# Latent attention: who copies the rotated queries, casts the keys and splits the sparse outputs, and where the first half projection stands

## The chip, the core and the metric

The kernel runs on one core of a Trainium2 chip. The metric is the device time of one execution in microseconds; below it is the median of several runs. The engines named are TensorE (PE; PEld is its weight load), VectorE (DVE), ScalarE (ACT), GpSimd (POOL) and SyncE (SP), which issues most DMAs. TensorE's clock has two levels, 1.2 and 2.4 GHz; the profile shows the granted one as a share of the higher.

## The reference, cut to what matters

The kernel computes two transformer blocks. The first has two layers of feed-forward, token mixer, feed-forward on 512 tokens of 1024 channels; the second is a mixer of another kind with routed experts, and is not touched. The change lies in the token mixer of the first block, in the latent attention (MLA) and in what follows it:

```python
def mla_attention(q_nope, q_pe, k_nope, k_pe, v):
    scale = (MLA_NOPE + MLA_ROPE) ** -0.5
        ...
        s = (jnp.einsum('bqhd,bkhd->bhqk', qn, k_nope, ...)
             + jnp.einsum('bqhd,bkd->bhqk', qp, k_pe, ...)) * scale
        s = jnp.where(kpos[None, :] <= qpos[:, None], s, NEG)
        p = jax.nn.softmax(s, axis=-1).astype(v.dtype)
        return jnp.einsum('bhqk,bkhd->bqhd', p, v)
```

There are 8 heads. A query or key of a head has 64 plain columns and 32 rotated ones; the rotated key columns are the same for all heads. The sparse attention (NSA) of the same mixer is done before. The outputs of both are then projected, multiplied by gates, added and projected once more.

## The kernel before

**Precision.** Products in 32 bits are made of three products of rounded parts. A tensor x is split into a high part, which is x rounded (whi, othi, mla_...), and a low part, which is x minus its high part (wlo, otlo). The product is lo·hi + hi·lo + hi·hi, so each product half of four column blocks is twelve matmuls (`products`, L424).

**Weights.** They come as blocks of 128x1024. SyncE loads a block into one of two `raw` buffers once GpSimd has split the one before the last. ScalarE casts it to `whi` (`hi`, L619, recorded at L624). GpSimd subtracts for `wlo` (`splitter`, L2967) and counts w_ready. TensorE waits for that count. GpSimd runs through its blocks in a fixed order, so whatever stands ahead of a split on its queue delays it.

**The hand-over.** The end of the mixer's first part makes the queries and keys of all heads from 14 tiles (`MLA_TILES`). VectorE takes those with even number, ScalarE those with odd number. Tiles 4 and 6 are the rotated parts of all queries; VectorE rotates them into q_rot (L1435 to L1438, L1618). After tile 10, VectorE subtracts for the low parts of head 0 (L1631 to L1633), copies tile 12 (L1622), and then lets TensorE and ScalarE pass a meeting point (`sync_point`, L412). Before TensorE reaches that point it does the first 12 matmuls of a gate block.

**The units.** Head and query tile make 32 units: 8 heads, and in each head four query tiles (qt 0 to 3) whose scores reach over 128, 256, 384 and 512 keys. Four functions walk through them, one for each engine, by the same counter u. TensorE (`pe_units_whole`) at step u first does three matmuls of a gate block (`feed`, L469), then the scores of unit u (L882 to L884), the transposes of the probabilities of unit u-2 (L892), and the product with the values of unit u-3 (L903). The gate matmuls end with u = 27. VectorE (`dve_units`) takes the maximum of unit u (L937) and its negative (L945), then whatever `next_head` adds, and after a whole head the reciprocal (L1666) and the division into o_mla (L1669). ScalarE (`act_units`) does the exponential of unit u (L913) and then the copy of the transposed probabilities of unit u-2 into p_mla (L923), then what its own `next_head` adds: parts of the next head, and after each eighth unit a weight cast (L624) and the copy of a finished gate (L479).

**The next head's parts.** While head h-1 runs, head h's high and low parts are made in one of two buffers, mla_even or mla_odd. ScalarE copies the head's 32 rotated query rows from q_rot into q_mla (L1394), casts the query (L1397) and the key (L1401). VectorE subtracts for the low parts (L1650). In the first two heads the shared rotated key rows are written as well (L1400, L1648); later heads find them in the buffer.

**The drain.** In the last four units VectorE also splits the four column blocks of the sparse output o_nsa, one behind each unit (`split_o`, L1660 and L1662). After the last product with the values TensorE does the first product half of the projection, that of the sparse output (`half(0, 1)`), then the transposes of o_mla (L1265), then the other halves.

## Time and profile before

| what | value |
|---|---|
| median of 3 runs | 2965.76 us (2962.89 to 2968.35) |
| the profiled execution | 2968.89 us, its span 2967.1 us |
| mean granted clock of TensorE in it | 0.985 |
| TensorE matmul | 2881.3 us, 97% |
| TensorE weight load | 2319.0 us, 78% |
| VectorE | 1519.0 us, 51% |
| ScalarE | 1213.1 us, 41% |
| GpSimd | 1174.8 us, 40% |

The first three rows of engines are busy times of one execution; busy does not mean at full clock. The latent-attention units of layer 0 run from about 646 to 721 us, those of layer 1 from about 1831 to 1909 us. In a timeline row a bracket tells how long the engine was idle before and what ended that.

### The profile page before, as it was taken

The numbers are of one execution on the slowest core, as the hardware profiler recorded it, in microseconds if no ns is written. First come the engines' busy times: TensorE is split into PE (matmuls) and PEld (weight loads), VectorE is DVE, ScalarE is ACT, GpSimd is POOL, SyncE is SP. The second block draws the span as 40 slices with busy tenths as digits, with TensorE's granted clock in tenths as the row PEclk, the third lists the DMA queues.
The fourth block names the chain that finished last, engine by engine and source line by source line (L and its number), as shares of the span: only waits on it lengthen the run. The fifth ranks groups of instructions, "written<-read, shape, count | busy, mean of one in ns | idle before, by whom it ended". The sixth has DMA issues, their size and how long they took to land.

```text
span 2967.1 us, 37748 instructions
## 1 busy us (share of the span) xinstructions
PE 2881.3 (97%) x13526; PEld 2319.0 (78%) x13526; DVE 1519.0 (51%) x2657; ACT 1213.1 (41%) x1857; POOL 1174.8 (40%) x594
## 2 busy tenths in 40 slices
PE   9999999999999999999999999999999999998997
PEld 7888888767888888788888876788888878776675
DVE  4441365555744413444136555574442579676675
ACT  4332233665343322433223366534332253535553
POOL 4444453521454443544435252145444443111331
PEclk9999999999999999999999999999999999999998
DMA  4323232202423332233323220242333212117995
GB/s 152 99 92 114 85 124 73 82 26 65 139 81 99 99 107 84 79 99 99 107 84 125 77 77 26 65 136 85 99 97 109 85 61 76 39 64 270 347 367 177
DMA packets 118574, 324.15 MB, mean 109 GB/s; under 512 B 12464, under 2 KB 48688, under 8 KB 117936
## 3 DMA queue, kind: packets, MB, share of 16 engines
q1 hardware_dynamic: 109024, 305.17, 31.6%
q10 hardware_dynamic: 2800, 8.91, 0.8%
q0 software_dynamic: 6624, 8.41, 0.8%
q8 instruction: 77, 1.26, 0.2%
q14 instruction: 49, 0.40, 0.0%
HBM read 313.52 MB, written 24.64 MB: 114 GB/s over the span
## 4 chain that ended last, share of the span: by engine, by line
PE 86%; DVE 7%; ACT 3%; issue 2%; DMA 1%; POOL 1%; DVEq 0%; SPq 0%; ACTq 0%; another core or an unknown queue 0%; POOLq 0%
PE ps L434 20%; PE ps L435 20%; PE ps L437 20%; PE ps L469 4%; PE ps L2204 3%; PE ps L1021 2%; PE ps L903 1%; PE ps L2190 1%; PE ps L2192 1%; PE ps L2191 1%; PE ps L1005 1%; PE ps L577 1%; PE ps L496 1%; PE ps L997 1%; PE ps L492 1%
## 5 line engine op out<-in xcount | busy, mean ns | idle before, releaser
L2967 POOL TENSOR_TENSOR wlo<-raw,whi 128x1024 fp32r<-128x1024 f32 (+1 forms) x368 | 954.4, 2595 | 1383.8 <-ACT whi L624 1383.7
L624 ACT ACTIVATE whi<-raw 128x1024 fp32r<-128x1024 f32 (+1 forms) x368 | 409.2, 1112 | 686.2 <-PE ps L437 579.4
L434 PE MATMUL ps<-xlo,whi 128*128 128x512 f32 x1704 | 665.2, 390 | 0.6 <-ACT gq L2240 0.6
L435 PE MATMUL ps<-xhi,wlo 128*128 128x512 f32 x1704 | 663.2, 389 | 0.0
L437 PE MATMUL ps<-xhi,whi 128*128 128x512 f32 x1704 | 420.8, 389 | 0.0
L434 PEld LDWEIGHTS ps<-xlo,whi 128*128 128x128 f32 x1704 | 320.0, 188 | 68.1 <-issue 1.7
L437 PEld LDWEIGHTS ps<-xhi,whi 128*128 128x128 f32 x1704 | 319.8, 188 | 66.4
L435 PEld LDWEIGHTS ps<-xhi,wlo 128*128 128x128 f32 x1704 | 319.8, 188 | 65.9
L434 PE MATMUL ps<-hlo,whi 128*128 128x512 f32 x704 | 277.3, 394 | 0.0
L435 PE MATMUL ps<-hhi,wlo 128*128 128x512 f32 x704 | 275.5, 391 | 0.0
L749 DVE SCALAR_TENSOR_TENSOR xa<-ps,xa 128x512 f32<-128x512 f32 x48 | 33.1, 689 | 353.2 <-PE ps L437 350.6
L709 DVE TENSOR_TENSOR hlo<-sg,hhi 128x512 f32 x88 | 203.7, 2314 | 10.8
L703 DVE TENSOR_TENSOR sg<-sg,ps 128x512 f32<-128x512 f32 x88 | 60.6, 688 | 290.2 <-PE ps L437 289.7
L699 DVE TENSOR_TENSOR sg<-sg,ps 128x512 f32<-128x512 f32 x88 | 60.5, 688 | 247.9 <-ACT sg L648 247.9
L437 PE MATMUL ps<-hhi,whi 128*128 128x512 f32 x704 | 171.5, 391 | 0.0
L434 PEld LDWEIGHTS ps<-hlo,whi 128*128 128x128 f32 x704 | 132.2, 188 | 29.7 <-issue 1.0
L435 PEld LDWEIGHTS ps<-hhi,wlo 128*128 128x128 f32 x704 | 132.2, 188 | 29.7 <-issue 1.0
L437 PEld LDWEIGHTS ps<-hhi,whi 128*128 128x128 f32 x704 | 132.2, 188 | 29.1
L648 ACT ACTIVATE sg<-ps 128x512 f32<-128x512 f32 x88 | 52.7, 598 | 192.6 <-PE ps L437 192.2
L2767 DVE TENSOR_TENSOR mlo<-mraw,mhi 128x2048 fp32r<-128x2048 f32 x46 | 103.4, 2288 | 37.3 <-ACT mhi L2365 37.3
L469 PE MATMUL ps<-xlo,whi 128*128 128x512 f32 x256 | 112.2, 438 | 2.0 <-DVEq L412 2.0
L648 ACT ACT_TABLE_LOAD x40 | 51.3, 1283 | 146.5 <-PE ps L437 145.5
(643 smaller groups left out, 4837.8 us busy)
## 6 DMA issues: line engine op xcount, KB each, us to landing
raw<-in_gu SPq DMA_DIRECT2D x176, 512.0 KB, 3.5
raw<-in_mix SPq DMA_DIRECT2D x96, 512.0 KB, 3.6
mraw<-in_w SPq DMA_DIRECT2D x23, 2048.0 KB, 17.2
raw<-in_dn SPq DMA_DIRECT2D x64, 704.0 KB, 4.0
mdraw<-in_w SPq DMA_DIRECT2D x23, 1024.0 KB, 15.6
raw<-in_w SPq DMA_DIRECT2D x32, 512.0 KB, 3.5
gate_rows<-tails SPq DMA_DIRECT2D x32, 256.0 KB, 4.2
sgmn<-gate_rows SPq DMA_DIRECT2D x16, 512.0 KB, 4.0
```

The costliest lines, as they stand in the source:

```text
L434: nc.tensor.matmul(out, whi[:, slot, cols], rlo, start=first and t == 0, stop=False)
L435: nc.tensor.matmul(out, wlo[:, slot, cols], rhi, start=False, stop=False)
L437: ins = nc.tensor.matmul(out, whi[:, slot, kk * P:kk * P + P], rhi, start=False, stop=last and t == n - 1)
L469: ins = nc.tensor.matmul(out, w[:, slot, t * P:t * P + P], x[:, t, :], start=k == 0, stop=k == 3 * KT - 1)
L624: nc.scalar.activation(whi[:, s, 0:n], raw[:, r, 0:n], ACT.Copy).then_inc(hi_done, 1)
L648: nc.scalar.activation(sg[:, j // 2 % 2, :], ps[UP_BANK[j % 4]][:], ACT.Sigmoid).then_inc(S["sig_ready"], 1)
L699: nc.vector.tensor_tensor(sg[:, j, :], sg[:, j, :], ps[UP_BANK[2 * j]][:], ALU.mult).then_inc(S["tile_free"], 1)
L703: nc.vector.tensor_tensor(sg[:, j, :], sg[:, j, :], ps[UP_BANK[2 * j + 1]][:], ALU.mult).then_inc(S["tile_free"], 1)
L709: nc.vector.tensor_tensor(hlo[:, bass.ds(i * 2 + j, 1), :], sg[:, j:j + 1, :], hhi[:, bass.ds(i * 2 + j, 1), :].bitcast(F32), ALU.subtract ...
L2204: ins = nc.tensor.matmul(ps[2 + half][:].rearrange("p (n c) -> p n c", n=4), hT[b % 2][:, j, :], mdraw[b % 3][:, 4 * half:4 * half + 4, j, ...
L2767: nc.vector.tensor_tensor(mlo[b % 4][:, :, k], mraw[b % 4][:, :, k], mhi[b % 2][:, :, k].bitcast(F32), ALU.subtract).then_inc(m_lo, 1)
L2967: nc.gpsimd.tensor_tensor(wlo[:, s, 0:n], raw[:, r, 0:n], whi[:, s, 0:n].bitcast(F32), ALU.subtract).then_inc(w_ready, 1)
```

## The change

There are four edits.

1. The copy of the rotated query rows moves from ScalarE to GpSimd. GpSimd does all seven at once, behind its work for the sparse attention and ahead of two weight splits. It waits for the semaphore q_turned, which VectorE raises in its tile 8 once both rotations have ended. Each copy waits for the one before. ScalarE's query cast waits for q_moved, the count of copies.
2. The cast of the key's high part moves, from head 2 on, from ScalarE to VectorE, just ahead of the subtraction that reads it.
3. The four splits of the sparse output move from the units 28, 29, 30 and 31 to the units 16, 20, 24 and 28.
4. The product half `half(0, 1)` moves from behind the last unit to step 33 of the units, between the product of unit 29 and the transposes of unit 31.

```diff
         def feed(u):
             pe_mla_gates(pe, L, MLA_LEAD + u * MLA_FEED, MLA_FEED)
+            if u == len(mla_units) + 1:
+                pe.wait_ge(S["v_ready"], 4)
+                pe.wait_ge(gate_raw, L * N_GATES + (N_GATES - 1))
+                pe.wait_ge(w_ready, L * G_LAYER + (G_PROJ + 1 + 2))
+                half(0, 1)
         pe_units_whole(pe, mla_units, nsa_bank, p_mla, s_ring, head, feed)
-        pe.wait_ge(S["v_ready"], 4)
-        pe.wait_ge(gate_raw, L * N_GATES + (N_GATES - 1))
-        pe.wait_ge(w_ready, L * G_LAYER + (G_PROJ + 1 + 2))
-        half(0, 1)
...
             if x == 0:
-                nc.scalar.activation(of[64:96], q_rot[32 * (h % 4):32 * (h % 4) + 32, h // 4, :], ACT.Copy
-                                     ).then_inc(S["kpe_copied"], 1)
-                act.wait_ge(S["kpe_copied"], h)
+                act.wait_ge(q_moved, 7 * L + h)
                 nc.scalar.activation(to, of, ACT.Copy).then_inc(S["qkhi_ready"], 1)
-            else:
-                if h < 2:
-                    nc.scalar.activation(to[64:96], k_pe[64:96, :], ACT.Copy)
+            elif h < 2:
+                nc.scalar.activation(to[64:96], k_pe[64:96, :], ACT.Copy)
                 nc.scalar.activation(to[0:64], of[0:64], ACT.Copy).then_inc(S["qkhi_ready"], 1)
...
+            if n == 8:
+                dve.wait_ge(S["rotated"], 2)
+                dve.sem_inc(q_turned, 1)
...
         def head_lo(h, x):
-            dve.wait_ge(S["qkhi_ready"], 2 * h + x + 1)
             if h >= 2:
                 dve.wait_ge(S["s_ready"], 4 * (h - 1))
             to, of = mla_part(h, x, 1)
+            if x and h >= 2:
+                nc.vector.tensor_copy(mla_part(h, x, 0)[0][0:64], of[0:64]).then_inc(S["qkhi_ready"], 1)
+            dve.wait_ge(S["qkhi_ready"], 2 * h + x + 1)
...
-            t = u - 28 + 4
-            if 4 <= t < 8:
-                split_o(t, o_nsa[:, t - 4, :])
+            if u % 4 == 0 and 16 <= u < len(mla_units):
+                split_o(u // 4, o_nsa[:, u // 4 - 4, :])
...
         pool_nsa(pool, L, one)
+        pool.wait_ge(q_turned, L + 1)
+        for h in range(1, 8):
+            nc.gpsimd.tensor_copy(q_mla[64:96, h, :], q_rot[32 * (h % 4):32 * (h % 4) + 32, h // 4, :]
+                                  ).then_inc(q_moved, 1)
+            pool.wait_ge(q_moved, 7 * L + h)
         for j in range(n + N_EARLY - NSA_GATES, len(MIX_AT)):
             one(L, G_MIX, 0, j)
```

GpSimd's queue where the sparse attention ends and the weight splits go on, before (wlo is the low part of a weight block, s_more one of four score buffers; line numbers after the change are one to three higher):

```order
L1063 TENSOR_SCALAR zs<-zs,small 128x512 [waits r_sum]
L1063 TENSOR_SCALAR s_more<-s_more,small 128x512 [waits r_sum]
L2967 TENSOR_TENSOR wlo<-raw,whi 128x1024 [waits hi_done] x22
L861 TENSOR_TENSOR xlo<-xa,xhi 128x512 [waits xa_ready] x8
L2967 TENSOR_TENSOR wlo<-raw,whi 128x1024 [waits hi_done]
```

And the same place now:

```order
L1064 TENSOR_SCALAR zs<-zs,small 128x512 [waits r_sum]
L1064 TENSOR_SCALAR s_more<-s_more,small 128x512 [waits r_sum]
L3010 COPY q_mla<-q_rot 32x512 [waits q_turned]
L3010 COPY q_mla<-q_rot 32x512 [waits q_moved] x6
L2970 TENSOR_TENSOR wlo<-raw,whi 128x1024 [waits hi_done,q_moved]
L2970 TENSOR_TENSOR wlo<-raw,whi 128x1024 [waits hi_done] x21
```

Seven copies stand ahead of all the weight splits that follow, and each waits.

TensorE's queue in the drain, from the product of unit 29 on, before (vm are the values, p_mla the transposed probabilities, othi and otlo the parts of the sparse output):

```order
L903 MATMUL ps<-vm_99,p_mla 128x64 [waits o_used,pthi_ready]
L903 MATMUL ps<-vm_99,p_mla 128x64
L892 MATMUL ps<-con,s_sb 128x128 [waits pthi_ready,p_ready]
L892 MATMUL ps<-con,s_sb 128x128 x3
L903 MATMUL ps<-vm_99,p_mla 128x64 [waits o_used,pthi_ready]
L903 MATMUL ps<-vm_99,p_mla 128x64
L903 MATMUL ps<-vm_100,p_mla 128x64
L903 MATMUL ps<-vm_99,p_mla 128x64 [waits o_used,pthi_ready]
L903 MATMUL ps<-vm_99,p_mla 128x64
L903 MATMUL ps<-vm_100,p_mla 128x64 x2
L434 MATMUL ps<-otlo,whi 128x512 [waits w_ready,gate_raw,v_ready]
L435 MATMUL ps<-othi,wlo 128x512
```

And now, from the same product on, with the middle of the product half left out:

```order
L904 MATMUL ps<-vm_99,p_mla 128x64 [waits o_used,pthi_ready]
L904 MATMUL ps<-vm_99,p_mla 128x64
L435 MATMUL ps<-otlo,whi 128x512 [waits w_ready,gate_raw,v_ready]
L436 MATMUL ps<-othi,wlo 128x512
...
L438 MATMUL ps<-othi,whi 128x512 x4
L893 MATMUL ps<-con,s_sb 128x128 [waits pthi_ready,p_ready]
L893 MATMUL ps<-con,s_sb 128x128 x3
L904 MATMUL ps<-vm_99,p_mla 128x64 [waits o_used,pthi_ready]
```

The twelve matmuls of the half now stand ahead of the transposes of the last unit, where they stood behind its product.

VectorE's queue in the last units, from the maximum of unit 29 on, before (o_nsa is the sparse output):

```order
L937 ISA zs,small<-ps,con 128x256 [waits pt_ready,s_ready]
L937 ISA small 128x1
L945 TENSOR_SCALAR small<-small 128x1 [waits dve_own]
L1660 CAST othi<-o_nsa 128x512
L1662 TENSOR_TENSOR otlo<-o_nsa,othi 128x512 [waits dve_own]
L937 ISA s_sb,small<-ps,con 128x384 [waits pt_ready,s_ready]
```

And now:

```order
L938 ISA zs,small<-ps,con 128x256 [waits pt_ready,s_ready]
L938 ISA small 128x1
L946 TENSOR_SCALAR small<-small 128x1 [waits dve_own]
L938 ISA s_sb,small<-ps,con 128x384 [waits pt_ready,s_ready]
L938 ISA small 128x1
```

The split between the two maxima is gone; that of unit 28 remains, and those of units 30 and 31 are gone likewise.

## Rows read from the trace of the kernel before

**Rows 1.** The page's busy times, shares of the span and instructions.

```profile
PE 2881.3 (97%) x13526; PEld 2319.0 (78%) x13526; DVE 1519.0 (51%) x2657; ACT 1213.1 (41%) x1857; POOL 1174.8 (40%) x594
```

**Rows 2.** Timeline (start, duration, engine, line, operation): first maximum of three heads, layer 0.

```profile
680.78 0.29 DVE L937 CUSTOM_DVE_ANT_0 s_sb<-ps,con 128x128 f32<-128x128 f32 x1
...
689.40 0.29 DVE L937 CUSTOM_DVE_ANT_0 zs<-ps,con 128x128 f32<-128x128 f32 x1
...
698.68 0.29 DVE L937 CUSTOM_DVE_ANT_0 s_sb<-ps,con 128x128 f32<-128x128 f32 x1
```

**Rows 3.** Timeline, layer 1, a gate head: a rotated copy, and TensorE's wait after it.

```profile
1860.91 0.63 ACT L1394 ACTIVATE q_mla<-q_rot 32x512 f32<-32x512 f32 x1
...
1864.66 1.10 PE L903 MATMUL ps<-vm,p_mla 128*128 128x64 f32 x8 [0.41 <-ACT p_mla L923]
```

**Rows 4.** Timeline of VectorE, layer 0: idle time before two maxima, and a cast.

```profile
683.13 0.42 DVE L937 CUSTOM_DVE_ANT_0 zs<-ps,con 128x256 f32<-128x256 f32 x1 [1.87 <-PE ps L884]
...
687.87 0.69 DVE L937 CUSTOM_DVE_ANT_0 s_sb<-ps,con 128x512 f32<-128x512 f32 x1 [1.04 <-PE ps L884]
...
707.62 0.42 DVE L1660 CAST othi<-o_nsa 128x512 fp32r<-128x512 f32 x1
```

**Rows 5.** Timeline of the drain of layer 0, TensorE and VectorE.

```profile
709.91 2.73 DVE L1662 TENSOR_TENSOR otlo<-o_nsa,othi 128x512 fp32r<-128x512 f32 x1
...
714.26 0.43 PE L903 MATMUL ps<-vm,p_mla 128*128 128x64 f32 x2 [1.11 <-ACT p_mla L923]
...
716.33 0.97 PE L903 MATMUL ps<-vm,p_mla 128*128 128x64 f32 x4 [1.30 <-ACT p_mla L923]
...
721.36 0.42 DVE L1669 TENSOR_TENSOR o_mla<-ps,small 128x256 f32<-128x256 f32 x1
...
723.90 1.08 PE L437 MATMUL ps<-othi,whi 128*128 128x512 f32 x4
...
724.82 1.91 PE L1265 MATMUL ps<-con,o_mla 128*128 128x128 f32 x16
```

**Rows 6.** Busy time in single microseconds: length, engines, granted clock, DMA share, GB/s.

```profile
716.00:717.00 1.00, 0.67 (x4) 0.67 (x5) 0.73 (x3) 0.66 (x3) 0.00 (x0) 0.76 0.12 39
...
723.00:724.00 1.00, 1.00 (x5) 0.80 (x4) 0.00 (x0) 0.00 (x0) 0.60 (x1) 0.82 0.00 0
...
2657.00:2658.00 1.00, 0.00 (x0) 0.00 (x0) 1.00 (x1) 0.60 (x1) 1.00 (x1) 1.00 1.04 422
...
2659.00:2660.00 1.00, 1.00 (x3) 0.76 (x3) 0.27 (x1) 0.64 (x2) 0.00 (x0) 0.50 1.07 378
```

**Rows 7.** Timeline of the hand-over of layer 0.

```profile
632.32 2.41 POOL L2967 TENSOR_TENSOR wlo<-raw,whi 128x1024 fp32r<-128x1024 f32 x1 [12.34 <-ACT whi L624]
...
632.85 2.42 DVE L1438 TENSOR_TENSOR sg<-sg,rope 128x512 f32<-128x512 f32 x1
...
638.02 0.69 DVE L1618 TENSOR_TENSOR q_rot<-q_rot,sg 128x512 f32<-128x512 f32 x1
...
639.54 2.38 POOL L2967 TENSOR_TENSOR wlo<-raw,whi 128x1024 fp32r<-128x1024 f32 x1 [4.81 <-ACT whi L624]
...
641.96 0.69 DVE L1631 TENSOR_TENSOR mla_odd<-q_mla,mla_odd 96x512 fp32r<-96x512 f32 x1 [1.34 <-ACT mla_odd L1386]
...
644.11 0.69 DVE L1622 COPY vm<-ps 128x512 f32<-128x512 f32 x1
...
645.51 0.49 PE L469 MATMUL ps<-xlo,whi 128*128 128x512 f32 x1 [0.99 <-DVEq L412]
```

**Rows 8.** Groups by form: GpSimd's operation with one tensor input, 512 columns.

```profile
L1063 POOL TENSOR_SCALAR s_sb<-s_sb,small 128x512 f32<-128x512 f32 x16 | 12.4, 773 | 12.7 <-DVE small L1083 12.7
```

**Rows 9.** Timeline: first maximum of either layer, and layer 1's transposes of the output.

```profile
646.79 0.29 DVE L937 CUSTOM_DVE_ANT_0 s_sb<-ps,con 128x128 f32<-128x128 f32 x1 [1.99 <-PE ps L884]
...
1832.29 0.29 DVE L937 CUSTOM_DVE_ANT_0 s_sb<-ps,con 128x128 f32<-128x128 f32 x1 [2.00 <-PE ps L884]
...
1912.84 1.91 PE L1265 MATMUL ps<-con,o_mla 128*128 128x128 f32 x16
```

More of the change, by code:

```diff
@@ L346, in program @@
     m_dyn = sem("m_dyn")
+    q_turned, q_moved = sem("q_turned"), sem("q_moved")
     conv_sums, conv_half = sem("conv_sums"), sem("conv_half")
@@ L1248, in head @@
                 pe.wait_ge(S["qklo_ready"], 2 * (u // 4) + 2)
-        def feed(u):
-            pe_mla_gates(pe, L, MLA_LEAD + u * MLA_FEED, MLA_FEED)
-        pe_units_whole(pe, mla_units, nsa_bank, p_mla, s_ring, head, feed)
         def half(m, s_, ready=None):
@@ L1255, in half, with feed @@
                                                for kk in range(4 * s_, 4 * s_ + 4)], ready=ready)
-        pe.wait_ge(S["v_ready"], 4)
-        pe.wait_ge(gate_raw, L * N_GATES + (N_GATES - 1))
-        pe.wait_ge(w_ready, L * G_LAYER + (G_PROJ + 1 + 2))
-        half(0, 1)
+        def feed(u):
+            pe_mla_gates(pe, L, MLA_LEAD + u * MLA_FEED, MLA_FEED)
+            if u == len(mla_units) + 1:
[3 more added lines that the diff above has]
+                half(0, 1)
+        pe_units_whole(pe, mla_units, nsa_bank, p_mla, s_ring, head, feed)
         pe.wait_ge(S["o_used"], 8)
```

## The prediction

> **What bounds the kernel now.** I read the busy shares first: TensorE is busy for 97% of the span [rows 1]. So only stretches in which TensorE stands, or runs at its lower clock, can give time back. Second, the list of waits and the timeline of the latent-attention units show where that is, from 646 us on in layer 0 and the same pattern again in layer 1. There the eight heads follow one another in two periods. From the first score of one head to that of the next it is 8.62 us (680.78 to 689.40), and 9.28 us (689.40 to 698.68) in a head in which ScalarE also casts a weight block and copies a gate [rows 2]. The longer head has one more wait of TensorE: the product of the fourth unit stands 0.41 us for the probabilities that ScalarE copies [rows 3]. Third, the drain behind the last head: TensorE stands 1.11 us and 1.30 us before two products, while VectorE does four splits, one of which takes 2.73 us beside a GpSimd split [rows 5]. Right behind that the granted clock falls: 0.76 in the mean of 716 to 717, 0.82 in the mean of 723 to 724, so half speed (1.2 in place of 2.4 GHz) from about 716.5 to 723.4, which costs 3.4 us of work [rows 6]. Fourth, the hand-over just before the units: TensorE stands 0.99 us at 645.51 for VectorE, whose last work is three subtractions and a copy from 641.96 to 644.80 [rows 7].
>
> **The change, part by part** (us per layer; both layers run it).
>
> *ScalarE loses the rotated copies and, from the third head on, the key cast.* Each copy takes 0.63 us in front of the query cast [rows 3], seven a layer. In the three gate heads that build a further head, that delays the fourth unit's probabilities, so at least the 0.41 us wait goes and at most the whole difference of 0.66 us between the periods [rows 2, 3]. I take 0.6: three heads, 1.8 us. In the plain heads nothing goes, since what remains there is the latency of score, maximum, exponential and copy. At the start of the units the copy also stands in front of the first query cast, while TensorE waits for the pipeline to fill: 0 to 0.63, taken 0.6. Sum of the units: 2.4 us.
>
> *VectorE gains the key cast and three earlier splits.* The nearest row of a cast is 0.42 us for 128x512 [rows 4]; the cast stands behind the third maximum, ahead of 1.04 us of idle time, so it is hidden. A split (0.42 + 0.69 us) after a head's first maximum stands ahead of 1.87 us of idle time, hidden too [rows 4]. Without that cover they would cost 6 x 0.42 and 3 x 1.1 us. So these edits cost nothing in the middle, and take three splits out of the drain, among them the one of 2.73 us [rows 5].
>
> *The drain.* The 1.11 us gap at 714.26 goes, since the maximum of the unit before last no longer queues behind the long split; its product then starts at 713.15. The 1.30 us gap before the next product stays, because the last unit's exponential still stands before the copy that it waits for. Then the work, at full clock: seven transposes by 0.12 (1.91 us for 16), the half projection with twelve products 0.23 apart (the row of four: 1.08 less 0.39, by three) or 2.8, eighteen products of probabilities and values by 0.14 (1.10 us for 8): 0.8 + 2.8 + 2.5 = 6.1 us [rows 3, 5]. The half projection no longer covers the reciprocal and the division of the last head: what stands between the last product and the transposes of the output is then bare, about 0.8 us (division 721.36 to 721.78, its reciprocal and two semaphores) [rows 5]. 713.15 + 1.30 + 6.1 + 0.8 is 721.4, against 724.82: 3.4 us, taken 3.3 for the small starts that I left out. If the clock falls in spite of this, its 3.4 us are lost again and the term is about zero; both ends are kept. The further product halves wait for weight blocks that are split long before. ScalarE's last copy, and with it the last weight cast, the store of the last gate and the loads of the gate rows, come no earlier; VectorE waits for these, but TensorE needs what VectorE then frees only four product blocks on, so I cost that at nothing.
>
> *GpSimd gains seven copies, and they stand in front of two weight splits.* This is what may cost. Before, GpSimd splits one block at 632.32 and one at 639.54, ending at 641.92, just as VectorE begins its three subtractions at 641.96 [rows 7]. Now it first waits for the second rotation. That rotation ended at 638.71; the multiplication that took 2.42 us beside the GpSimd split will take 0.69, since no split runs there, so it ends 1.73 earlier, at 637.0 [rows 7]. The copies then start between 637.0 and 637.6. No such copy is in the trace; the nearest row is GpSimd's operation with one tensor input, 0.77 us for 512 columns [rows 8]. With 0 to 0.2 us for the wait on its own semaphore, seven take 5.4 to 6.9 us and end between 642.4 and 644.5, and the two splits of 2.4 us follow. So all three subtractions of VectorE now have GpSimd work beside them, and the trace shows what an operation with two SBUF inputs does beside a split: 2.42 in place of 0.69 us. Whether a copy does the same is not in the trace: from nothing to its whole 0.77 us. I take the whole, as the only row of such a meeting shows a full wait. If the copies last through the subtractions, each of these waits for one: 0.1 to 0.7, then about 0.6 and 0.6, which is 1.3 to 1.9, taken 1.5 us. TensorE waits for just that, so its gap grows from 0.99 to 2.5 us. After a gap like that (nothing ran in 2657) the clock stood at 0.50 in 2659 [rows 6]. In layer 1 the clock already falls soon after the hand-over: from the first maximum to the output's transposes layer 1 takes 2.5 us longer than layer 0 (1832.29 to 1912.84, against 646.79 to 724.82) [rows 5, 9]. So I add a fall in layer 0 alone, 1.7 us, about half of the 3.4 of the drain's fall, as at half clock the fill's gaps are hidden.
>
> The Trainium skill, SBUF — State Buffer, section "Who interferes with whom", says that a VectorE instruction with two SBUF inputs contends with a GpSimd instruction that reads SBUF, and that the second to issue is blocked for the whole of the first. By that rule the copies hold the subtractions as the split does, and the 1.5 us stand; the trace agrees for the split (2.42 against 0.69 us) and has no copy.
>
> GpSimd's splits also come some 8 us later, and with them the loads behind them on the sync queue. The first is needed by the gate products of the second head, some 5 us behind the hand-over, so I cost that at nothing.
>
> **Sum.** 2 x (2.4 + 3.3 - 1.5) = 8.4, less 1.7 for the clock, is 6.7 us. Against the profiled execution's 2968.89 that is 2962.2; the median of the runs shown lies 3.13 lower, and I carry that over: 2965.76 - 6.7 = 2959.1, said as 2959.
>
> **The rivals.** (a) *GpSimd's copies do not hold VectorE.* For it: no row shows such a meeting. Then 2 x 5.7 = 11.4 us go: 2954.4, and 2952 if layer 1's early clock fall goes as well (2.5). (b) *A split lands between the subtractions, or the drain's clock falls again.* If the copies are done by 643.5, the first split takes the pair ahead of the last subtraction: 0.4 + 0.6 + 2.2 is 3.2 us. 2 x (5.7 - 3.2) - 1.7 = 3.3 us, 2962.5. If instead the clock falls behind the 1.30 us gap that is left, the forecast loses 3.4 in one layer or both: 2962.5 or 2966. (c) *Slower.* If the copies are quicker than 0.7 us and done before 641.96, both splits stand between the subtractions: 2 x 2.25, or 4.5 us. TensorE then stands 5.5 us, the clock falls for as long as in layer 1 (2.5 us, in layer 0 now too), and if it also falls in the drain, 2 x 3.4 go: 2 x (5.7 - 4.5) - 2.5 - 6.8 is -6.9, 2972.7. It decides from the point at which the longer gap and the clock together take over 5.7 us a layer. Against it: GpSimd's one-input row would have to be 0.1 too long for a copy. (d) *The change doesn't do what it says*, because ScalarE is not what the gate heads wait for: then the units give nothing, 2959 + 4.8 = 2964; it goes with (b).
>
> **How the numbers follow.** Forecast 0.40, (a) 0.20, (b) with (d) 0.27, (c) 0.13. A measurement of this kernel tells 0.2% (5.9 us) from no change. The forecast's own range is 2955 to 2963, by the ends of its terms, so of its 0.40 some 0.25 lie below 2959.8; with (a) and a little of (b), faster is 0.47. Slower is nearly all of (c), 0.12. Same is 0.41. The range runs from 2952, the low end of (a), to 2970, inside (c).
>
> **What would show it.** Right: seven GpSimd copies of about 0.77 us between 637 and 644.5; the three subtractions longer than 0.69; TensorE's gap at the hand-over over 2 us; gate heads at about 8.7 us; no gap over 0.4 us at the product of the first drain unit; a granted clock of 1.0 through the drain; the half projection between two products of the drain. Wrong: subtractions of 0.69 us in a row (a), one of 2.9 (b) or two (c), gate heads still at 9.28 (d), a clock under 0.8 in the drain. What would make it wrong altogether is VectorE becoming late for the maxima in the middle, with gaps ahead of the scores that were not there.

## The result: slower by 0.4%, and where the time went

The changed kernel takes 2980.86 us (median of 6 runs, 2978.0 to 2985.52), the kernel before 2969.09 us beside it (6 runs, 2962.89 to 2972.68). The ratio is 1.004, with a 95% interval of 1.003 to 1.005. The forecast was 2959 us, 2952 to 2970, so it missed in sign and in range. The profiled execution took 2980.70 us with a span of 2978.9 us, against 2968.89 us before: 11.81 us more.

The page's busy line shows nothing of it. TensorE does the same work, and its share is again 97% [rows 1]:

```profile
PE 2885.7 (97%) x13526; PEld 2323.7 (78%) x13526; DVE 1525.1 (51%) x2669; ACT 1196.5 (40%) x1831; POOL 1182.1 (40%) x608
```

Marks that stand in both traces show it. I took four in each layer: VectorE's first subtraction of head 0, the first maximum of the units, the first transpose of the output o_mla, and VectorE's first sum behind the output projection's first pair of blocks (L750, before L749). The differences of their starts:

| stretch | before, layer 0 / 1 | after, layer 0 / 1 | difference |
|---|---|---|---|
| first subtraction to first maximum (hand-over) | 4.83 / 4.84 | 9.87 / 9.88 | +5.0 / +5.0 |
| first maximum to output transposes (units, drain) | 78.03 / 80.55 | 73.71 / 74.08 | -4.3 / -6.5 |
| output transposes to that sum (projection) | 53.93 / 53.77 | 59.34 / 59.35 | +5.4 / +5.6 |

They sum to +10.3 us; the last 1.5 us lie outside the mixer's second half. So the units and the drain give about what was forecast, and two places of about 5 us a layer take it back. Of layer 1's 6.5 us, 2.5 are no work of the change: the second head of the kernel before took 12.02 us there, at a granted clock of 0.50 from 1842 to 1846 us, and 9.51 us in layer 0.

**The hand-over.** The timeline of GpSimd around it, and under it VectorE's and TensorE's (start, duration, engine and line; the bracket is the idle time before). They answer [rows 7]:

```profile
635.27 4.62 POOL L3010 COPY q_mla<-q_rot 32x512 f32<-32x512 f32 x7 [17.13 <-DVEq L1628]
639.98 5.14 POOL L2970 TENSOR_TENSOR wlo<-raw,whi 128x1024 fp32r<-128x1024 f32 x2
640.16 2.76 DVE L1633 TENSOR_TENSOR mla_odd<-q_mla,mla_odd 96x512 fp32r<-96x512 f32 x1 [1.87 <-ACT mla_odd L1388]
642.95 2.71 DVE L1634 TENSOR_TENSOR mla_odd<-k_pe,mla_odd 32x512 fp32r<-32x512 f32 x1
645.70 0.68 DVE L1635 TENSOR_TENSOR mla_odd<-k_mla,mla_odd 64x512 fp32r<-64x512 f32 x1
647.81 0.79 PE L470 MATMUL ps<-xlo,whi 128*128 128x512 f32 x1 [5.10 <-DVEq L413]
```

Seven copies take 4.62 us, 0.66 us each. They are done at 639.89, and both weight splits follow at once. VectorE's first subtraction comes at 640.16, so one split meets the first subtraction and the other the second: 2.76 and 2.71 us in place of 0.69, and TensorE stands 5.10 us instead of 0.99. That is 4.1 of the 5.0 us. The other 0.9 are half clock behind the gap (length, busy time, granted clock, DMA share, GB/s):

```profile
648.00:652.00 4.00, 4.00 (x13) 0.50 0.06 24
```

**The units.** VectorE's first maximum in the same three heads as [rows 2]:

```profile
683.51 0.29 DVE L938 CUSTOM_DVE_ANT_0 s_sb<-ps,con 128x128 f32<-128x128 f32 x1
692.11 0.29 DVE L938 CUSTOM_DVE_ANT_0 zs<-ps,con 128x128 f32<-128x128 f32 x1
700.71 0.29 DVE L938 CUSTOM_DVE_ANT_0 s_sb<-ps,con 128x128 f32<-128x128 f32 x1
```

The gate head (692.11 to 700.71) now takes 8.60 us instead of 9.28, as long as a plain one.

**The drain.** TensorE's rows that answer [rows 5] (the last transposes of the sixteen are cut off), and its clock there:

```profile
713.11 1.10 PE L904 MATMUL ps<-vm,p_mla 128*128 128x64 f32 x8 [0.45 <-ACT p_mla L924]
717.05 0.66 PE L904 MATMUL ps<-vm,p_mla 128*128 128x64 f32 x4 [1.37 <-ACT p_mla L924]
720.80 1.96 PE L904 MATMUL ps<-vm,p_mla 128*128 128x64 f32 x14
723.74 1.06 PE L1267 MATMUL ps<-con,o_mla 128*128 128x128 f32 x7 [0.98 <-DVEq L1681]
716.00:720.00 4.00, 2.95 (x15) 1.00 0.49 175
720.00:724.00 4.00, 2.95 (x24) 1.00 0.00 0
```

The gap of 1.11 us is gone, that of 1.30 stays (1.37), and the bare division costs 0.98 us. The clock, which was 0.57 and 0.58 in these two stretches before, stays up.

**Behind the drain.** ScalarE's rows from its last copy of probabilities, SyncE's issues (SPq) and TensorE's wait at the output projection's first pair, 50 us later:

```profile
721.00 0.60 ACT L924 ACTIVATE p_mla<-ps 128x512 f32<-128x512 f32 x1 [3.62 <-PE ps L893]
722.91 1.06 ACT L625 ACTIVATE whi<-raw 128x1024 fp32r<-128x1024 f32 x1
726.43 0.33 SPq L2962 DMA_DIRECT2D raw<-in_mix  x1
726.81 0.52 SPq L2977 DMA_DIRECT2D gate_rows<-tails  x1
731.11 0.90 SPq L2987 DMA_DIRECT2D sgmn<-gate_rows  x2
735.15 1.06 ACT L1412 ACTIVATE sgmn<-sgmn 128x1024 f32<-128x1024 f32 x1 [9.89 <-DMA sgmn<-gate_rows]
774.99 0.51 PE L1289 MATMUL ps<-ylo,whi 128*128 128x512 f32 x1 [2.35 <-DVE ylo L1700]
```

In the kernel before, the same ScalarE rows stood here (L1413 is L1412 now):

```profile
718.19 0.60 ACT L923 ACTIVATE p_mla<-ps 128x512 f32<-128x512 f32 x1 [1.53 <-PE ps L892]
732.28 1.06 ACT L1413 ACTIVATE sgmn<-sgmn 128x1024 f32<-128x1024 f32 x1 [9.82 <-DMA sgmn<-gate_rows]
```

This is a chain: the last copy, the last weight cast on ScalarE, its split on GpSimd, the load that waits for the split on the sync queue, behind it the store of the last gate, then the fetch of the gate rows, the sigmoids, and VectorE's gate products, down to ylo. The half projection now stands ahead of the last unit's transposes, so the last copy waits 3.62 us instead of 1.53. In the trace's time the chain comes 2.9 us later and the output's transposes 1.1 us earlier (723.74 against 724.82). Counted from the first maximum of the units, which takes the hand-over out, the last copy stands where it stood (70.97 us behind it against 71.40), and the transposes come 4.3 us earlier. So TensorE has moved and the chain has not. Before, TensorE's rows show no wait for ylo; now it waits 2.35 us in layer 0 and 3.6 us in layer 1. TensorE's busy time and clock in layer 0, right behind the transposes and around that wait (length, busy time, granted clock, DMA share, GB/s):

```profile
724.00:728.00 4.00, 4.00 (x20) 0.57 0.16 24
770.00:774.00 4.00, 2.64 (x12) 1.00 0.45 150
774.00:778.00 4.00, 3.01 (x8) 0.71 0.44 135
778.00:782.00 4.00, 4.00 (x17) 0.87 0.22 82
```

The wait, 2.35 us, and what the three falls take at most (0.43, 0.29 and 0.13 of 4 us, 3.4 us together) make up the stretch's +5.4 us. The first fall lies ahead of the wait and only shortens it: layer 1 reaches the pair without such a fall, waits 3.6 us, and its stretch is as long (59.35 us).

### The profile page after: what moved, and what is told of

It is laid out like the page before. It is cut to its first block and busy times, and to the rows that moved or that the text cites. A ratio compares the mean times of both kernels' runs of the same rounds, so it can differ in the third digit from the quotient of the medians.

```text
span 2978.9 us, 37764 instructions
## 1 busy us (share of the span) xinstructions
PE 2885.7 (97%) x13526; PEld 2323.7 (78%) x13526; DVE 1525.1 (51%) x2669; ACT 1196.5 (40%) x1831; POOL 1182.1 (40%) x608
## 5 line engine op out<-in xcount | busy, mean ns | idle before, releaser
L750 DVE SCALAR_TENSOR_TENSOR xa<-ps,xa 128x512 f32<-128x512 f32 x48 | 33.1, 689 | 356.1 <-PE ps L438 350.3
L710 DVE TENSOR_TENSOR hlo<-sg,hhi 128x512 f32 x88 | 203.6, 2313 | 10.8
L470 PE MATMUL ps<-xlo,whi 128*128 128x512 f32 x256 | 111.6, 436 | 10.2 <-DVEq L413 10.2
## 6 DMA issues: line engine op xcount, KB each, us to landing
mdraw<-in_w SPq DMA_DIRECT2D x23, 1024.0 KB, 16.4
```

What stands on the lines that cost most here:

```text
L470: ins = nc.tensor.matmul(out, w[:, slot, t * P:t * P + P], x[:, t, :], start=k == 0, stop=k == 3 * KT - 1)
L710: nc.vector.tensor_tensor(hlo[:, bass.ds(i * 2 + j, 1), :], sg[:, j:j + 1, :], hhi[:, bass.ds(i * 2 + j, 1), :].bitcast(F32), ALU.subtract ...
```

## The experiments

Times are differences of medians against the kernel before, run beside; the change itself stands at +11.8 us. Theory H blames the hand-over, theory G the chain of the gate rows, theory V VectorE's new work.

**1. The copies back on ScalarE.**

```diff
-                act.wait_ge(q_moved, 7 * L + h)
+                nc.scalar.activation(of[64:96], q_rot[...], ACT.Copy).then_inc(S["kpe_copied"], 1)
+                act.wait_ge(S["kpe_copied"], h)
 ...
 (and GpSimd's wait and seven copies, and VectorE's q_turned, taken out)
```

> The changed kernel with the rotated copies back on ScalarE; casts, splits and the half inside the drain stay as changed. All times against the kernel before (the changed kernel stands at +11.8 us). Theory H (the hand-over pays it all: GpSimd's copies push both weight splits onto VectorE's three subtractions, 4.1 us of gap and about 1 us of half clock per layer): the gap at the hand-over is 1.0 us again, 10 us come back, less about 1 us a layer that the copies cost ScalarE: 0 to +4 us. Theory G (the half ahead of the last transposes puts ScalarE's last copy 2.8 us later, and through the last weight cast, its split, the last gate's store and the gate rows the output projection's wait for ylo, 2.35 and 3.6 us, plus a clock fall behind it): the wait at the output projection's first pair stays over 2 us, and +5 to +9 us remain. Theory V (VectorE's casts and splits in the middle of the units are what costs): over +9 us.

Measured: +3.2 us (ratio 1.0013, 1.0004 to 1.0022). The hand-over's gap is 1.0 us again, and 8.6 us come back, as H says. But TensorE still waits for ylo, 2.3 and 4.6 us, as G says. V is out.

**2. The half behind the last unit again, GpSimd's copies kept.**

```diff
-            if u == len(mla_units) + 1:
-                (waits)
-                half(0, 1)
         pe_units_whole(pe, mla_units, nsa_bank, p_mla, s_ring, head, feed)
+        (waits)
+        half(0, 1)
```

> The changed kernel with the projection half back behind the last unit; GpSimd's copies, VectorE's casts and the spread splits stay. Against the kernel before (changed kernel: +11.8 us). Theory H (hand-over alone): the gap of 5.1 us stays at the hand-over, and the half's gain in the drain is lost, so +12 to +18 us. Theory G (gate rows late because of the half): ScalarE's last copy comes 2.8 us earlier relative to the last unit, the wait for ylo at the output projection falls under 0.5 us, and 2 x (2.35 + 1.7) less what the drain loses (about 2 us a layer) gives +6 to +9 us. Theory V: no change, +11 to +13 us.

Measured: +5.4 us (1.0021, 1.0012 to 1.003). The time was below H's range and just below G's, and G's mechanism failed as stated: TensorE waits 2.6 and 4.8 us for ylo, though ScalarE's last copy is no longer held up. Units and drain took 72.8 and 72.6 us, less than with the half inside (73.7 and 74.1). The drain alone, from the first maximum of the last head to the output's transposes, took 17.6 us in both layers of the kernel before, 14.5 in the changed kernel and 13.35 here, with layer 0's clock at 1.00 in the last two. So the drain's gain comes with the spread splits, 3.4 us of it with the clock that stays up, and the half's new place costs 1.1 us a layer: behind the last unit the half covers the division, which is bare in the changed kernel.

**3. Casts and spread splits alone.**

```diff
 (edits of experiments 1 and 2 together)
```

> Only VectorE's key casts and the three spread splits are kept; copies on ScalarE and the half behind the last unit, as before. Against the kernel before. Theory H and theory G agree here: nothing that either blames is left, the gate heads lose 0.42 us of ScalarE's time each and the drain loses the wait of 1.11 us and the long split: -3 to -6 us. Theory V (VectorE's extra work in the middle costs): +3 us or more, with waits of TensorE in the units that the kernel before has not.

Measured: -0.3 us (0.9998, 0.9988 to 1.0007). A miss for both. The drain's long gap is gone, but in layer 1 TensorE then waits for ylo, in a kernel that has neither the copies on GpSimd nor the half in the drain. The list of TensorE's waits there (total, times, longest) has:

```profile
PE ps L1287 <- DVE ylo L1697: 2.6, 1, 2.6
```

The two layers differ in the drain's clock. In layer 0 it falls (0.52 from 716 to 720 us), the drain takes 16.4 us, and there is no wait for ylo. In layer 1 it stays at 1.00, the drain takes 13.35 us, and the wait is there. So the half clock in the drain of the kernel before, 3.4 us, also hid the chain.

Against experiment 2 this prices the hand-over with GpSimd's copies, less what they give the units, at 5.7 us.

**4. As experiment 1, with the half one step later** (behind the last transposes, ahead of the last product).

```diff
-            if u == len(mla_units) + 1:
+            if u == len(mla_units) + 2:
```

> Copies on ScalarE; VectorE's casts and splits kept; the half stands one unit step later than in the changed kernel, behind the last unit's transposes and ahead of its last product, so it no longer delays ScalarE's last copy. Beside the run with the half one step earlier this differs by that step alone. Theory G: ScalarE's last copy, and with it the gate rows, come about 2.8 us earlier, the wait for ylo falls under 0.5 us and the clock stays up at the output projection, so this one is 5 to 9 us faster than the run with the half one step earlier, at -4 to -8 us against the kernel before. Theory H: the step makes no difference beyond 1 us a layer between the two runs, since the half only fills a gap in either place.

Measured: +0.5 us (1.0001, 0.9992 to 1.001), 2.7 us faster than experiment 1. TensorE does not wait for ylo any more, so G's link is right; but in the median the forecast gain did not come. The profiled execution took 2964.05 us, 6.1 us under that median and inside G's range, so its trace can't show where the rest of the median went. Even in it the clock falls in layer 0's second head: it is 0.73 and 0.59 in the two stretches from 650 to 660 us, and 1.00 in experiment 3, whose rows there are the same work. What decides that fall the runs don't tell.

**What the first four say together.** G had the wrong variable. Whether TensorE waits goes with how long after the output's transposes the first sigmoid starts, whichever of the two moved:

| kernel | first sigmoid after the first transpose, layer 0 / 1 | wait for ylo, layer 0 / 1 |
|---|---|---|
| before | 7.5 / 7.5 | 0 / 0 |
| after | 11.4 / 11.1 | 2.3 / 3.6 |
| 1 copies on ScalarE | 11.5 / 11.6 | 2.3 / 4.6 |
| 2 half behind | 9.6 / 9.5 | 2.6 / 4.8 |
| 3 casts and splits only | 6.2 / 10.2 | 0 / 2.6 |
| 4 half later | 7.4 / 7.3 | 0 / 0 |
| 5 (below) | 8.4 / 10.2 | 0.9 / 6.0 |
| 6 (below) | 7.6 / 7.7 | 0.2 / 0 |
| 7 (below) | 7.7 / 7.7 | 0 / 0 |

Up to 7.7 us the wait is 0.2 us or less, from 8.4 us on it is there. How long it is does not follow from this number alone (10.2 us gave 2.6 and 6.0). The kernel before stood at 7.5 us. How near to a wait that is, its own rows show: VectorE's seventh low part ylo of layer 0 and the matmul of the first pair that takes it, and above them one of the products that lead to such a part, beside a weight split.

```profile
757.43 2.41 POOL L2967 TENSOR_TENSOR wlo<-raw,whi 128x1024 fp32r<-128x1024 f32 x1 [2.76 <-ACT whi L624]
757.92 2.48 DVE L1691 TENSOR_TENSOR sgmn<-sgmn 128x512 f32<-128x512 f32 x1
771.49 0.69 DVE L1697 TENSOR_TENSOR ylo<-sgmn,yhi 128x512 f32 x1
772.24 0.50 PE L1287 MATMUL ps<-ylo,whi 128*128 128x512 f32 x1
```

The part is done at 772.18 and taken at 772.24; in layer 1 it is done 0.4 us ahead. So the room was between nothing and 0.4 us. Any edit that lets TensorE come to the transposes earlier uses that up, unless the chain comes earlier too. One reason why VectorE is that late stands in the first two rows: six of its first seven products at L1691 take 2.4 to 2.8 us in place of 0.69, each beside a GpSimd split.

**5. GpSimd's copies behind the two splits, the half one step later.**

```diff
         for j in range(n + N_EARLY - NSA_GATES, len(MIX_AT)):
             one(L, G_MIX, 0, j)
+            if j == n + N_EARLY - NSA_GATES + 1:
+                pool.wait_ge(w_ready, L * G_LAYER + (G_MIX + j + 3))
+                (wait for q_turned and the seven copies, from ahead of the loop)
```

> GpSimd's seven copies stand behind the two weight splits that used to come before the units (so these splits run at their old times, 632 and 639.5 us in layer 0), and the half stands one step later, behind the last transposes; casts and splits as changed. The copies now begin at about 642 us, just when VectorE begins its three subtractions. Theory H (the splits were the price, not the copies as such): if a one-input copy of 0.66 us does not hold VectorE, the gap at the hand-over is 1.0 us as before; if it does, each subtraction waits for one copy, 1.3 to 1.9 us more, gap 2.3 to 2.9 us; in either case far from 5.1 us. Against the run with copies on ScalarE and the half in this place (+0.5 us against the kernel before) the units gain 2 x 1.7 us: -3 us against the kernel before without holding, 0 to +1 us with it. Rival (GpSimd's copies cost by themselves, wherever they stand, by later loads or by holding VectorE in full): +4 us or more.

Measured: 0.0 us (0.9998, 0.9989 to 1.0007). At the hand-over H holds: TensorE's gap is 1.6 us. GpSimd and VectorE there (the seven copies as one row, then the first two by themselves):

```profile
642.09 5.84 POOL L3014 COPY q_mla<-q_rot 32x512 f32<-32x512 f32 x7
642.09 1.12 POOL L3014 COPY q_mla<-q_rot 32x512 f32<-32x512 f32 x1
643.28 0.95 POOL L3014 COPY q_mla<-q_rot 32x512 f32<-32x512 f32 x1
642.06 0.69 DVE L1633 TENSOR_TENSOR mla_odd<-q_mla,mla_odd 96x512 fp32r<-96x512 f32 x1 [1.36 <-ACT mla_odd L1388]
642.78 0.98 DVE L1634 TENSOR_TENSOR mla_odd<-k_pe,mla_odd 32x512 fp32r<-32x512 f32 x1
643.79 0.98 DVE L1635 TENSOR_TENSOR mla_odd<-k_mla,mla_odd 64x512 fp32r<-64x512 f32 x1
```

Copies and subtractions take turns. The second subtraction begins while the first copy runs and ends 0.55 us behind that copy's end (643.76 against 643.21); the third ends 0.54 us behind the second copy's end. Beside a split of the kernel before it was the same (635.27 against 634.73, [rows 7]). So a copy holds a subtraction until it is done, as a split does. It costs only 0.29 us (0.98 less 0.69), not its whole 0.66, because part of the copy is over when the subtraction comes, and the subtraction needs 0.55 and not 0.69 us from there. The units and the drain took 72.5 and 73.5 us, 5.5 and 7.1 less than before; nearly all of it was lost again behind the drain, where the stretch grew by 1.1 and 9.2 us, with waits for ylo of 0.9 and 6.0 us.

**6. The changed kernel with one exchange on the sync queue:** the store of the last gate ahead of the load that waits for the last split.

```diff
+            if late == N_GATES - N_EARLY - 1:
+                store(N_EARLY + late)
             loader(sp, d["mix"], j - at_, 8, G_FFN2 - G_MIX)(L, G_MIX, 0, at_)
-            if 0 <= late < N_GATES - N_EARLY:
+            if 0 <= late < N_GATES - N_EARLY - 1:
                 store(N_EARLY + late)
```

> The changed kernel with one step of the sync queue exchanged: the store of the last gate stands ahead of the load that waits for the last weight split, not behind it. Nothing on TensorE, VectorE, ScalarE or GpSimd is moved. In the changed kernel that store left at 726.81 us though its data were ready at 712.1, and the gate rows were fetched at 731.1. Theory G (the half delays ScalarE's last copy and so the cast, the split, the store and the gate rows): the gate rows are fetched at about 727, the output projection's wait for ylo (2.35 us in layer 0, 3.6 in layer 1) falls under 0.5 us, its clock stays up, and 2 x (2.4 to 4) us come back: +4 to +7 us against the kernel before instead of +11.3. The hand-over's gap of 5.1 us stays. Rival (the ylo wait comes from VectorE's own queue, not from the gate rows): the wait stays over 2 us, +10 to +12 us.

Measured: +1.6 us (1.0004, 0.9995 to 1.0013), so about 10 us of the change's loss come back, more than I expected. Up to the output's transposes (723.76 against 723.74 us) the trace is that of the changed kernel, the gap of 5.1 us at the hand-over included. Then SyncE, ScalarE and TensorE:

```profile
714.47 1.18 SPq L2977 DMA_DIRECT2D gate_rows<-tails  x2
726.95 0.90 SPq L2987 DMA_DIRECT2D sgmn<-gate_rows  x2
731.36 1.06 ACT L1412 ACTIVATE sgmn<-sgmn 128x1024 f32<-128x1024 f32 x1 [6.06 <-DMA sgmn<-gate_rows]
771.59 0.50 PE L1289 MATMUL ps<-ylo,whi 128*128 128x512 f32 x1 [0.24 <-DVE ylo L1700]
```

The rows are fetched 4.2 us earlier, the wait falls from 2.35 to 0.24 us, and the projection's stretch takes 54.3 and 54.0 us instead of 59.3. That settles the second place: it is the chain.

**7. Both repairs on the changed kernel** (the copies of 5, the store of 6, the half where the change put it).

> The changed kernel with both repairs: GpSimd's copies behind the two splits, and the store of the last gate ahead of that load; the half stays where the change put it, ahead of the last transposes. Theories H and G together: the hand-over's gap is 1.0 to 2.9 us, no wait for ylo over 0.5 us, the units gain 2 x 1.7 us and the drain 2 x 3 us: -4 to -9 us against the kernel before. If either theory misses its half of the loss, +3 us or more remains.

Measured: -7.8 us (0.9976, 0.9966 to 0.9986), inside the forecast of both theories together. The repair of the hand-over is worth 9.4 us (against 6), that of the store the other 10.2 of the 19.6 us between the changed kernel and this one.

**8. The kernel before with the store moved, as a control.**

> The kernel before with nothing changed but the sync queue's step: the store of the last gate ahead of the load that waits for the last weight split. It is the control for the version with both repairs (-7.8 us). If the gate rows were already what the output projection of the kernel before waited for, with TensorE in its way, the step gives -3 us or more here too. If the kernel before had TensorE as its bound there (its trace shows no wait for ylo over 0.3 us), the rows come 4.3 us earlier and nobody needs them: -1 to +1 us, and the 7.8 us are the change's own edits.

Measured: +0.6 us (0.9999, 0.999 to 1.0008). The first sigmoid comes 2.7 us behind the output's transposes instead of 7.5, and nobody needs it: the projection's stretch takes 53.8 us in both layers, as before. So the 7.8 us are the change's own edits.

**9. As 7, with the copies on ScalarE.**

> Casts, splits, the half inside the drain and the store moved ahead; the rotated copies back on ScalarE. Against the version with both repairs (-7.8 us) only the copies differ: GpSimd's copies behind the two splits cost 0.6 us at the hand-over and give 1.7 us in the units, 2 x 1.1 us a run. Theory G and the forecast's units term: -4 to -6.5 us against the kernel before; if ScalarE was not what the gate heads wait for, -8 to -9 us.

Measured: -6.6 us (0.9974, 0.9962 to 0.9985). GpSimd's copies are worth about 1 us by the medians; the intervals of 7 and 9 overlap, so the times do not show it. The trace does: with the copies on ScalarE the two gate heads of layer 0 take 9.29 and 9.28 us, in 7 they take 8.61 and 8.60.

**10. As 7, with the half one step later.**

> Both repairs, with the half one step later (behind the last transposes). Theory G: with the store ahead the gate rows no longer hang on ScalarE's last copy, so where the half stands no longer matters: -7 to -9 us, within 2 us of the version with both repairs. Without the store moved this kernel stood at 0.0 us, with waits of 0.9 and 6.0 us for ylo, which must be gone. Rival (the half's place matters by itself, by the clock in the drain): over 2 us apart, in either direction.

Measured: -11.7 us (0.9959, 0.9946 to 0.9973), 3.9 us below 7, with overlapping intervals. The waits for ylo are gone, as expected. The division's 0.98 us is bare in both, but the clock is 1.00 from 720 to 728 us of layer 0, against 0.74 and 0.83 in 7. That the half's place causes this is not shown; in layer 1 of this execution the drain takes 15.7 us for 14.1 in layer 0.

**11. As 7, with the copies begun only behind VectorE's subtractions.**

```diff
-            if n == 8:
-                dve.wait_ge(S["rotated"], 2)
-                dve.sem_inc(q_turned, 1)
 ...
         own.wait()
+        dve.wait_ge(S["rotated"], 2)
+        dve.sem_inc(q_turned, 1)
```

> Both repairs, and GpSimd's copies begin only when VectorE is through with the subtractions, at about 645 us in layer 0. In the version with both repairs two of the three subtractions took 0.98 in place of 0.69 us beside copies, and TensorE's gap was 1.6 in place of 0.99 us. If the copies hold VectorE, the subtractions take 0.69 us again, the gap is 1.0 us, and 2 x 0.6 us go: -8 to -10 us. If the 0.98 has another cause, the gap stays 1.6 us. If the first copy comes too late for the second head's query cast, the units' first gaps grow and it is slower than -7 us.

Measured: -9.1 us (0.997, 0.9957 to 0.9982). VectorE's two subtractions and TensorE's gap behind them:

```profile
641.02 0.68 DVE L1631 TENSOR_TENSOR mla_odd<-k_pe,mla_odd 32x512 fp32r<-32x512 f32 x1
641.74 0.68 DVE L1632 TENSOR_TENSOR mla_odd<-k_mla,mla_odd 64x512 fp32r<-64x512 f32 x1
643.80 0.49 PE L470 MATMUL ps<-xlo,whi 128*128 128x512 f32 x1 [0.94 <-DVEq L413]
```

So the 0.98 us were the copies' doing.

**12. All of it:** the store first, the copies last, the half one step later.

> Everything that the runs so far favour at once: casts and spread splits on VectorE, GpSimd's copies begun behind VectorE's subtractions, the store of the last gate ahead of that load, the half one step later. With the copies a step earlier this kernel stood at -11.7 us against the kernel before, and the copies' step took the gap at the hand-over from 1.6 to about 1 us: -10 to -14 us, the gap 1.0 us, no wait for ylo over 0.5 us. Rival (the difference of 3.9 us between the two places of the half was chance, and the copies' step is worth nothing): -8 to -9 us, as the other versions with both repairs.

Measured: -14.1 us (2955.92 us, 2955.15 to 2956.95, against 2970.06 us; ratio 0.9953, 0.9939 to 0.9966). This is faster than the kernel before, timed beside it; the changed kernel was 11.8 us slower than the kernel before. From 640 to 800 us, TensorE's waits are these, with none for ylo:

```profile
PE ps L904 <- ACT p_mla L924: 5.7, 11, 1.4
PE ps L1267 <- DVEq L1680: 1.0, 1, 1.0
PE ps L470 <- DVEq L413: 0.9, 1, 0.9
PE ps L435 <- DVE xa L750: 0.2, 1, 0.2
```

No run has the half behind the last unit together with the store moved. The drain takes 14.1 us in both layers here and 13.35 with the half behind (experiment 2), so an estimate from these two is that 0.8 us a layer are left.

## Why the prediction was wrong

**The units: right, with one head counted too many.** Forecast were 2.4 us a layer. From the first maximum of head 0 to that of head 7 in layer 0 the kernel before takes 60.43 us (646.79 to 707.22), and experiment 12, whose clock is full there, 58.38 (648.20 to 706.58): 2.05 us. Two gate heads give 0.68 each (9.28 to 8.60), the fill 0.46 (the first head, 6.58 to 6.12); the third gate head, 9.51 before, gives 0.06. In the changed kernel it is 59.22, since the clock was at half in the first head (7.05). The gain is that of the rotated copies alone: with the key cast moved and the copies left (experiment 3) the span is 60.42 us.

**VectorE's new work: right.** Casts and splits are hidden: in the changed kernel TensorE waits for p_mla and for the bare division from the first maximum of layer 0 to the transposes, and for nothing else (5.1 and 1.0 us; for p_mla 8.2 before).

**The drain: right, though not by the half.** Forecast were 3.3 us a layer, measured 3.1 (17.6 to 14.5). The steps stand in the rows: the gap of 1.11 gone, 1.37 for 1.30, 0.98 for 0.8, and above all the clock at 1.00 from 716 to 724 us, as the forecast said. The half has no share in it: the forecast charged its move with the bare division, and experiment 2, without the move, gains 4.25 us. Units and drain together gave 10.8 us for a forecast of 11.4; part of that nearness is luck, since the 2.5 us of half clock that layer 1 no longer has and the 0.9 and 1.4 us of half clock that the first heads got are about even.

**The hand-over: the mis-sized term.** It was sized at 1.5 us a layer, with copies of 0.77 to 0.98 us that would still run during the three subtractions (seven of the longest are 6.8 us, not 6.9, which changes nothing). They began where the forecast had them, 4.9 us ahead of the first subtraction. But their duration came from a GpSimd row of other work, 128x512 with one tensor input [rows 8]. A copy of 32x512 takes 0.66 us with its wait, so all seven end 0.27 us before the first subtraction, and the two splits meet the first two subtractions. That is rival (c)'s first half, point for point: it asked for copies quicker than 0.7 us and gave a gap of 5.5 us; 5.10 was measured. I gave (c) 0.13 because its point of decision lay 0.1 us below a row that was no row of a copy. With the bound at 0.7 and the only price at 0.77 from a larger operation, both sides deserved like chances. The cost: 5.0 us a layer, 10.1 in all, for a forecast of 4.7 (2 x 1.5 and 1.7 of clock). The clock fell in both layers, not in layer 0 alone: 0.9 us of it lie in this stretch, 0.9 and 1.4 more in the first head. Nor was the price of copies beside the subtractions right: where they do meet (experiment 5), the gap grows by 0.6 us, not 1.5.

**The chain of the gate rows: the step that failed.** The forecast saw it: ScalarE's last copy, the last cast, the store and the loads "come no earlier; VectorE waits for these, but TensorE needs what VectorE then frees only four product blocks on, so I cost that at nothing". The first half held: counted from the first maximum of layer 0, the last copy comes 0.4 us earlier (with the half behind, in experiment 2, it comes 3.0 us earlier, so the half's new place ate that). The second half failed. A distance of four blocks is no slack when VectorE reaches its end no sooner than TensorE: before, the seventh part was ready 0.06 us (layer 0) and 0.4 us (layer 1) ahead of its use, and the forecast itself took 3.3 us by making TensorE earlier. Had I followed the chain to its last reader in the trace, the room would have stood there. The cost is 11.0 us in both layers, for a forecast of nothing; moving the store alone brings 10.2 back (experiment 6), and the same step gives nothing in the kernel before (experiment 8).

**The sum.** Forecast -11.4 (units and drain) + 4.7 (hand-over and its clock) + 0 (chain) = -6.7 us; measured -10.8 + 10.1 + 11.0 = +10.3 us, and 1.5 us elsewhere.

**The page of the Trainium skill that the prediction weighed.** The Trainium skill, SBUF — State Buffer, "Who interferes with whom", has the second of the two instructions blocked until the first is through. The trace agrees for the splits and for the copies: a VectorE operation that begins beside either ends 0.54 to 0.55 us behind the end of the GpSimd instruction (experiment 5 and [rows 7]). What failed was not the rule but the price that the forecast drew from it. It let each subtraction wait for a whole copy; the copy had itself been held by the subtraction before, and part of it was over.

## What to carry to other kernels

Before you count a stretch of the bounding engine as saved, find who it meets next, and how late that one already is: here a chain over four engines and a queue ended at most 0.4 us ahead of its use, and the gains ahead of it were lost until one store was moved in the queue. A copy put "in idle time" on another engine moves all that is queued behind it; ask what the pushed work will then stand beside. If a rival's point of decision lies within the error of a borrowed duration, give it as much chance as the forecast.

## What the runs showed of the hardware

- A GpSimd copy of 32x512 in 32 bits takes 0.61 us alone, 0.66 with its wait for the one before (seven in 4.62 us), and 0.95 to 1.12 beside a VectorE subtraction (experiment 5).
- A VectorE operation of 0.69 us with two inputs in SBUF that begins beside a GpSimd instruction ends 0.54 to 0.55 us behind the end of that instruction, be it a split of two tensors (2.42 us, [rows 7]) or a copy of one (0.98 us, experiment 5).
- The half-clock stretches come and go between kernels that do the same work at the place: right behind the first transposes of the output the clock was 0.57 in the changed kernel and 1.00 in experiment 6 (724 to 728 us), whose TensorE comes there within 0.02 us of the other's time. The largest here cost 3.4 us (the drain of the kernel before), and no run here says what sets them off. One place is regular: behind the hand-over's gap of 5.1 us the first head ran in part at half clock in all six layers that have that gap (7.0 to 7.6 us long), behind gaps of 1.6 us in three of six, and behind gaps of 0.9 to 1.0 us in none of sixteen (6.1 to 6.6 us).
